# Adding each expert block into the output rows in DRAM, in place of a combination behind the blocks

## The reference, cut to what matters

```
g_sel = argmax(g_logits)                       # 1 of 4 groups
top_p, top_i = top_k(softmax(e_logits), 2)     # 2 of the group's 8 experts
top_w = g_gate * top_p / sum(top_p)
...                                            # assignments sorted by expert, padded to blocks of 128 rows
def expert_rows(xb, e):
    hid = silu(xb @ w_gate[e]) * (xb @ w_up[e])      # 1024 -> 512
    return hid @ w_down[e]                           # 512 -> 1024
y_rows = map(expert_rows, x_rows, block_expert)
y = zeros.at[row_token].add(y_rows * row_weight)     # every token is in two blocks
out = h + y
```

## Time and profile before

| | |
|---|---|
| median of three runs | 1733.02 us |
| profiled execution | 1731.12 us, span 1729.0 us |
| mean granted TensorE clock | 0.962 |
| busy share of the span | PE 93%, DVE 72%, ACT 37%, POOL 21% |
| expert blocks | about 1061 to 1691 us |
| combination (L1622 to L1626) | about 1691 to 1729 us |

### The profile page before, as it was taken

One profiled execution on the slowest core, in us unless ns is written; L12 is line 12 of the kernel. 1 busy time (PEld: TensorE's weight loads), 2 busy tenths in 40 slices (PEclk: granted clock), 3 DMA queues, 4 the chain that ended last, 5 costly groups with the idle time before them and its releaser, 6 DMA issues. The chain is left out here.

```text
span 1729.0 us, 25257 instructions
## 1 busy us (share of the span) xinstructions
PE 1599.6 (93%) x7334; PEld 1254.7 (73%) x7334; DVE 1253.2 (72%) x2272; ACT 640.1 (37%) x1075; POOL 360.5 (21%) x495
## 2 busy tenths in 40 slices
PE   6999999999999999999998854999999999999991
PEld 5778888788888788888887744667766776677660
DVE  6658878768688587787786747767776777677655
ACT  5333232223232322332322412545554555455430
POOL 2221121221221211303221011222122212211210
PEclk9999999999999999999999966999999999999996
DMA  4221221221221211212213533799999999999927
GB/s 149 52 74 44 56 68 44 56 68 33 66 55 56 62 36 51 73 38 68 56 49 122 211 127 103 285 358 353 359 370 353 355 364 359 348 346 349 356 101 297
DMA packets 138508, 292.62 MB, mean 169 GB/s; under 512 B 17920, under 2 KB 68528, under 8 KB 137392
## 3 DMA queue, kind: packets, MB, share of 16 engines
q1 hardware_dynamic: 129056, 274.68, 45.7%
q0 software_dynamic: 9360, 16.80, 2.7%
HBM read 283.42 MB, written 25.30 MB: 179 GB/s over the span
## 5 line engine op out<-in xcount | busy, mean ns | idle before, releaser
L1691 ACT ACTIVATE gu_hi<-w_gu 128x1024 fp32r<-128x1024 f32 x256 | 272.6, 1066 | 311.3 <-PE g_ps L1734 247.4
L1788 DVE TENSOR_TENSOR gu_lo<-w_gu,gu_hi 128x1024 fp32r<-128x1024 f32 x256 | 313.4, 1225 | 90.6 <-ACT gu_hi L1691 67.2
L1027 PE MATMUL proj<-uTh,wl 128*128 128x512 f32 x768 | 309.6, 403 | 6.9 <-issue 6.9
L1029 PE MATMUL proj<-uTh,wh 128*128 128x512 f32 x768 | 301.8, 393 | 0.0
L1028 PE MATMUL proj<-uTl,wh 128*128 128x512 f32 x768 | 301.5, 393 | 0.0
L1752 PE MATMUL y<-w_d,hT 128*128 128x512 f32 x512 | 225.1, 592 | 1.0 <-DVE hT L1814 1.0
L450 POOL TENSOR_TENSOR wl<-raw,wh 128x512 fp32r<-128x512 f32 x96 | 128.7, 1358 | 393.1 <-ACT wh L511 393.1
L1752 PEld LDWEIGHTS y<-w_d,hT 128*128 128x128 f32 x512 | 94.9, 190 | 108.4 <-issue 107.1
L1027 PEld LDWEIGHTS proj<-uTh,wl 128*128 128x128 f32 x768 | 145.8, 190 | 37.3 <-issue 7.5
L1029 PEld LDWEIGHTS proj<-uTh,wh 128*128 128x128 f32 x768 | 145.4, 189 | 31.6
L1028 PEld LDWEIGHTS proj<-uTl,wh 128*128 128x128 f32 x768 | 145.8, 190 | 28.7
(11 more groups left out here) (244 smaller groups left out, 2733.8 us busy)
## 6 DMA issues: line engine op xcount, KB each, us to landing
w_gu<-in_moe_w_gate_dram SPq DMA_DIRECT2D x128, 512.0 KB, 8.8
w_gu<-in_moe_w_up_dram SPq DMA_DIRECT2D x128, 512.0 KB, 9.2
w_d<-in_moe_w_down_dram SPq DMA_DIRECT2D x128, 512.0 KB, 5.6
raw<-in_ssd_w_in_dram SPq DMA_DIRECT2D x96, 256.0 KB, 3.5
E<-acum_dram SPq DMA_DIRECT2D x64, 256.0 KB, 3.6
raw<-in_ssd_w_out_dram SPq DMA_DIRECT2D x32, 256.0 KB, 3.0
w_gu<-y_dram SPq DMA_DIRECT2D x8, 1024.0 KB, 9.8
hacc<-in_x_dram SPq DMA_DIRECT2D x8, 512.0 KB, 7.2
```

What stands on the lines that cost most here:

```text
L1027: nc.tensor.matmul(out, al, bh, start=start, stop=False)
L1029: return nc.tensor.matmul(out, ah, bh, start=False, stop=stop)
L1691: nc.scalar.activation(wh[:, j % RING, :], weights.gate_up(b, j), ACT.Copy).then_inc(w_hi, 1)
L1788: vec.tensor_tensor(wl[:, j % RING, :], weights.gate_up(b, j), wh[:, j % RING, :].bitcast(F32), ALU.subtract).then_inc(w_lo, 1)
```

## The change: rows are fetched, added to and stored back, block by block

- `routing` gets `hacc` and `out`, and SP stores the eight tiles of `hacc` to `out` there, ahead of the eight down-weight loads. `ridx` keeps one index per row, the token; the second value carried through the table is now the row's weight (`wrow`).
- A new `fetch` on GpSimd reads block m's rows of `out` into `yb` by an indirect DMA. Its index operations come right behind the scatter of block m-1; the DMA waits until that scatter has landed, since both blocks may hold the same token.
- `y_out` becomes two additions `yb = y * wrow + yb`, waits for the fetch, and moves in VectorE's program: block m's now stands in the pass of block m+2, behind the low parts of pieces 4 to 7. In the last pair the one of block 30 stands ahead of the last `hT` copy, the one of block 31 at the very end.
- `scatter` writes `yb` to the rows of `out`. The combination is gone; the program ends when the last scatters have landed.

```
 def routing(...):
         def _(sp):
             ...
+            ov = out.rearrange("(i p) d -> p i d", p=P)
+            for i in range(NT):
+                sp.dma_start(ov[:, i, :], hacc[:, i, :]).then_inc(out_stored, 16)
             ...
+            g.memset(yb[:], 0.0).then_inc(const_steps, 1)
-            link(vec.tensor_tensor(wtok[:, 0, :], s8[:, 3, :], s8[:, 10, :], ALU.mult))
-            link(vec.tensor_tensor(wtok[:, 1, :], wtok[:, 0, :], s8[:, 7, :], ALU.mult))
+            link(vec.tensor_tensor(src[:, 0, :, 1], s8[:, 3, :], s8[:, 10, :], ALU.mult))
+            link(vec.tensor_tensor(src[:, 1, :, 1], src[:, 0, :, 1], s8[:, 7, :], ALU.mult))
             for k in range(2):
                 link(vec.tensor_scalar(src[:, k, :, 0], toki[:], -PADROW, None, ALU.add))
-                link(vec.tensor_scalar(src[:, k, :, 1], toki[:], 2.0, k - PADROW, ALU.mult, ALU.add))
...
-            link(vec.tensor_scalar(ridx[:], tab_ps[:], PADROW, None, ALU.add))
+            link(vec.tensor_scalar(ridx[:], tab_ps[:, 0, :], PADROW, None, ALU.add))
+            link(vec.tensor_copy(wrow[:], tab_ps[:, 1, :]))
 def experts(...):
             last = pairs(sp, body, peeled=2)
             load_down(last, 1)
-            for b in range(2):
-                sp.wait_ge(scattered[b], val(last, 0, 8, 16))
-            ...                                  # loads of y_dram, stores of hacc
-            def scatter(p, b):
-                wait(pool, scattered[b], p, 0, 8, 0)
-                g.tensor_copy(stmp[:, b, :], ridx[:, 1, bass.ds(val(p, b, 1, 0), 1)]).then_inc(sidx_done, 1)
+            def fetch(p, b):
+                g.tensor_copy(stmp[:, b, :], ridx[:, bass.ds(val(p, b, 1, 0), 1)]).then_inc(sidx_done, 1)
                 wait(pool, sidx_done, p, b, 3, 1)
-                wait(pool, y_done, p, b, 2, 2)
                 g.tensor_tensor(sidx[:, b, :], stmp[:, b, :], zero[:], ALU.add).then_inc(sidx_done, 1)
                 wait(pool, sidx_done, p, b, 3, 2)
+                if b == 1:
+                    wait(pool, scattered[0], p, 0, 8, 16)
+                else:
+                    wait(pool, scattered[1], p, 0, 8, 0)
                 g.tensor_tensor(held[:, 1, :], zero[:], zero[:], ALU.add).then_inc(sidx_done, 1)
-                g.indirect_dma_start(y_dram, bass.IndirectOffsetOnAxis(sidx[:, b, :].bitcast(U32), 0), yb[:, b, :], None,
-                                     bounds_check=last_row, oob_is_err=False).then_inc(scattered[b], 16)
+                g.indirect_dma_start(yb[:, b, :], None, out, bass.IndirectOffsetOnAxis(sidx[:, b, :].bitcast(U32), 0),
+                                     bounds_check=last_token, oob_is_err=False).then_inc(fetched[b], 16)
+            def scatter(p, b):
+                wait(pool, y_done, p, b, 2, 2)
+                g.tensor_tensor(held[:, 2, :], zero[:], zero[:], ALU.add).then_inc(held_done, 1)
+                g.indirect_dma_start(out, bass.IndirectOffsetOnAxis(sidx[:, b, :].bitcast(U32), 0), yb[:, b, :], None,
+                                     bounds_check=last_token, oob_is_err=False).then_inc(scattered[b], 16)
...
                         scatter(shifted(p, -1), 1)
+                    fetch(p, b)
...
             def y_out(p, b):
-                wait(dve, scattered[b], p, 0, 8, 0)
+                wait(dve, fetched[b], p, 0, 8, 16)
                 for j in range(2):
                     wait(dve, y_mm, p, b, 2, j + 1)
-                    vec.tensor_copy(yb[:, b, j * 512:(j + 1) * 512], y_ps[j][:]).then_inc(y_done, 1)
+                    rows = yb[:, b, j * 512:(j + 1) * 512]
+                    vec.scalar_tensor_tensor(rows, y_ps[j][:], wrow[:, bass.ds(val(p, b, 1, 0), 1)], rows,
+                                             ALU.mult, ALU.add).then_inc(y_done, 1)
             def body(p, last):
                 for b in range(2):
                     for j in range(RING, 8):
                         split(p, b, j)
+                    if p[0] is not None or p[1]:
+                        y_out(shifted(p, -1), b)
...
-                    if b == 1:
+                    if b == 1 and last:
                         y_out(p, 0)
-                    elif p[0] is not None or p[1]:
-                        y_out(shifted(p, -1), 1)
...
-            for i in range(NT):                  # additions into hacc
-                ...
```

More of the change, by code:

```diff
@@ L1224, in _, with routing @@
                 logits(k)
-def routing(nc, lg, ridx, etab, npairs, wtok, weights, xg, zero, ident, b_group, b_expert):
+def routing(nc, hacc, lg, ridx, wrow, etab, npairs, weights, xg, yb, zero, ident, b_group, b_expert, out, out_stored):
     NT = lg.shape[1]
@@ L1485, in _, with experts @@
             dve.wait_ge(tab_mm, 2 * NT)
-            link(vec.tensor_scalar(ridx[:], tab_ps[:], PADROW, None, ALU.add))
-def experts(nc, hacc, ridx, etab, npairs, wtok, weights, xg, zero, ident, u2_dram, y_dram, out):
+            link(vec.tensor_scalar(ridx[:], tab_ps[:, 0, :], PADROW, None, ALU.add))
+            link(vec.tensor_copy(wrow[:], tab_ps[:, 1, :]))
+def experts(nc, T, ridx, wrow, etab, npairs, weights, xg, yb, zero, ident, u2_dram, out, out_stored):
     _, D, FF = weights.src[0].shape
@@ L1497, in experts @@
     KF = FF // P
-    NT = hacc.shape[1]
-    T = NT * P
+    NT = T // P
     RING = 4
@@ L1522, in experts @@
         stmp = sb("stmp", [P, 2, 1], I32)
-        held = sb("held", [P, 2, 1], I32)
+        held = sb("held", [P, 3, 1], I32)
         tp = [psum(f"tp3_{j}", [P, 4, P]) for j in range(2)]
@@ L1528, in experts @@
         y_ps = [psum(f"y3_{j}", [P, 512]) for j in range(2)]
-        y2 = [weights.gu[j // 2][:].rearrange("p a k f -> p (a k f)")[:, (j % 2) * 2 * D:(j % 2 + 1) * 2 * D]
-              .rearrange("p (c d) -> p c d", c=2) for j in range(4)]
         w_hi = sem("w_hi3")
@@ L1538, in experts @@
         sidx_done = sem("sidx_done")
+        held_done = sem("held_done")
         gathered = [sem(f"gathered{b}") for b in range(2)]
+        fetched = [sem(f"fetched{b}") for b in range(2)]
         scattered = [sem(f"scattered{b}") for b in range(2)]
@@ L1549, in experts @@
         y_done = sem("y_done3")
-        y2_loaded = [sem(f"y2_loaded{j}") for j in range(4)]
-        comb = sem("comb")
-        out_stored = sem("out_stored")
         def val(p, b, per, add):
@@ L1630, in _ @@
             g = nc.gpsimd
-            last_token, last_row = pool.to_reg(T - 1), pool.to_reg(2 * T - 1)
+            last_token = pool.to_reg(T - 1)
             def gather(p, b, ahead):
@@ L1638, in gather @@
                 wait(pool, turned, p, b, 2, 2 * (ahead - 1))
-                g.tensor_copy(gtmp[:, par, :], ridx[:, 0, bass.ds(val(p, b, 1, ahead), 1)]).then_inc(gidx_done, 1)
+                g.tensor_copy(gtmp[:, par, :], ridx[:, bass.ds(val(p, b, 1, ahead), 1)]).then_inc(gidx_done, 1)
                 wait(pool, gidx_done, p, b, 3, 3 * ahead + 1)
@@ L1668, in body @@
                         scatter(shifted(p, -1), 1)
+                    fetch(p, b)
             for ahead in range(3):
                 gather(FIRST, 0, ahead)
+            pool.wait_ge(out_stored, 16 * NT)
             last = pairs(pool, body, peeled=2)
@@ L1675, in _ @@
             pool.wait_ge(gathered[0], val(last, 0, 8, 32))
+            for b in range(2):
+                pool.wait_ge(scattered[b], val(last, 0, 8, 16))
         @block.scalar
@@ L1819, in _ @@
             y_out(pairs(dve, body, peeled=2), 1)
-            for i in range(NT):
-                dve.wait_ge(y2_loaded[i % 4], 16 * (i // 4 + 1))
-                for c in range(2):
-                    if c:
-                        dve.wait_ge(comb, 2 * i + 1)
-                    vec.scalar_tensor_tensor(hacc[:, i, :], y2[i % 4][:, c, :], wtok[:, c, i:i + 1], hacc[:, i, :],
-                                             ALU.mult, ALU.add).then_inc(comb, 1)
 def layer(nc, x, norm_mix, norm_ffn, ssd_w_in, ssd_conv_w, ssd_conv_b, ssd_dt_bias, ssd_a_log, ssd_d, ssd_norm,
@@ L1846, in layer @@
         xg = ctx.enter_context(nc.sbuf_tensor("xg", [P, 2, D], F32))
+        yb = ctx.enter_context(nc.sbuf_tensor("yb", [P, 2, D], F32))
+        out_stored = ctx.enter_context(nc.semaphore("out_stored"))
         zero = ctx.enter_context(nc.sbuf_tensor("zero", [P, 1], I32))
         ident = ctx.enter_context(nc.sbuf_tensor("ident2", [P, P], F32))
-        routing(nc, lg, ridx, etab, npairs, wtok, weights, xg, zero, ident, moe_b_group[0], moe_b_expert[0])
-        experts(nc, hacc, ridx, etab, npairs, wtok, weights, xg, zero, ident, u2_dram, y_dram, out[0])
+        routing(nc, hacc, lg, ridx, wrow, etab, npairs, weights, xg, yb, zero, ident, moe_b_group[0], moe_b_expert[0],
+                out[0], out_stored)
+        experts(nc, T, ridx, wrow, etab, npairs, weights, xg, yb, zero, ident, u2_dram, out[0], out_stored)
 _INS = ["x", "norm_mix", "norm_ffn", "ssd_w_in", "ssd_conv_w", "ssd_conv_b", "ssd_dt_bias", "ssd_a_log", "ssd_d",
```

8 lines of the change are left out of this document (3 added, 5 removed).

## The result

| | before | changed |
|---|---|---|
| median | 1732.64 us (20 runs, 1728.51 to 1736.33) | 1739.02 us (20 runs, 19 of them 1731.09 to 1745.94) |
| profiled execution | 1731.12 us, span 1729.0 | 1732.48 us, span 1730.7 |
| mean period of the additions, blocks 1 to 26 | 19.15 us (TensorE's pass) | 20.26 us |
| last `y` product starts | 1683.28 us | 1709.51 us |

The ratio is 1.0032, with a 95% interval of 1.0019 to 1.0044. I had forecast 1702 us, a gain; the time lies outside the range. One run of the changed kernel stands apart, at 5881.53 us: it is left out of the ratio and of the range, and without it the median is 1738.95. The changed kernel's runs also spread more than those of before (15 us against 8, without that one), and its profiled execution is the second shortest of them, 6.5 us under the median.

A forecast was written before the change was run, and what follows sets the result against it. TensorE was taken to bound the blocks, with 38 us of combination behind them. Removing it, with a hidden ring, a new tail and 0.3 less routing, gave span 1698.1 against 1729.0, gain 30.9, median 1702 us; range 1697 to 1728.

The forecast's parts named there:

- The bound: In the blocks: TensorE, busy 198.00 of 198.00 us, sets the 19.15 us pass; behind them 38 us of combination without matmuls.
- the ring: Once per block: additions, scatter, next fetch, next additions; length L 18.32 us, under the 19.15 us pass, so no cost.
- the price of a microsecond (28 us): In the blocks: each microsecond of L over 19.15 costs 28 us, for 28 blocks beside weight loads, less 1.94 once.
- fetch: the same form as the gather, median 6.5: Last transfer of the loop: the fetch lands after 6.5 us, the gathers' median of 4.5 / 6.5 / 7.6.
- the other four terms: Rest of the loop: additions 1.49, to scatter's instruction 1.59, to fetch's `held` 8.19, to fetch's instruction 0.50 us.
- the first rival: Blocks: fetch issued at the pass's start takes 8.1, L 19.9, 20 us lost, time 1722; chance 0.20 for binding in part.
- the 16.6 at which the prediction said that the whole gain goes: Blocks: scatter and fetch landings summing to over 15.5 us cost something; over 16.6 they take the whole gain.
- the slower rival: Blocks: both transfers at slow ends, 10.2 and 7.6, L 21.5, 65 us lost, time 1767; chance 0.12.
- 0.4 to the end: Tail: the span ends 0.4 us after the last scatter lands at 1698.0, so at 1698.4.
- `held` and the additions: In the pass: `held` ahead of the scatter 1.19 us beside low parts; the two additions 1.49 us.
- Routing and the stores: Stage ahead of the blocks: about -0.3 us; the eight `hacc` stores, 10 us, hidden with 11 us to spare.
- VectorE's cover of 1.94 us: In a pass: 1.94 us are left for a late fetch before TensorE stands still.

The follow-up runs named there:

- lengthening the ring: Changed kernel with four more 128x1 POOL operations between the scatter's landing and the fetch; 1767.91 us, ratio 1.0202 to the kernel before.
- other rows: Changed kernel with all its waits, but the fetch reads the same number of rows from `u2_dram`; 1738.58 us, ratio 1.0034 to the kernel before.
- last wait on SyncE: Changed kernel with the waits for the last two scatters on SP instead of POOL, and a 512-byte store behind them; one execution, 1740.04 us.
- gather ahead of the fetch: Changed kernel with POOL's gather of block m+3 moved behind the scatter of m-1, ahead of the fetch of m; 1723.09 us, ratio 0.9941.
- fetch freed: Changed kernel, but the fetch reads `u2_dram` and waits only for its buffer, the scatter of two blocks ago; 1706.92 us, ratio 0.985.
- groups in turn, additions between: Changed kernel with blocks from the four expert groups in turn, fetch waiting for the scatter of m-2 up to block 27; 1707.11 us, ratio 0.9871.
- `hid` and longer: Changed kernel with additions behind product `hid` in the pass of block m+1 and four added POOL operations before the fetch; 1726.75 us, ratio 0.997.
- four groups in turn, with the additions behind `hid`: Changed kernel with additions behind `hid`, last waits on SP, blocks from the groups in turn, looser fetch wait up to block 27; 1705.70 us, ratio 0.9843.

## Why the prediction was wrong, step by step

- **The bound, and the ring.** Right in kind. The pieces, their order and the price of a microsecond (28 us) are as forecast; freeing the fetch and lengthening the ring show it from both sides. By the prediction's own rule the measured period costs 28 x (20.26 - 19.15) - 1.9 = 29.2 us; 27.4 were found.
- **The step that failed: "fetch: the same form as the gather, median 6.5".** It measures 9.1 with its wake, 2.6 more, while the other four terms came out 0.6 shorter together. L is 20.26 and not 18.32. The row was right for the gather of before, which started 14.0 us into TensorE's pass (a median, counted from the first gate matmul). The fetch starts 2.3 us into it. I had given this as the first rival, with 8.1 for the fetch, and set it aside because the gathers land after 6.5 in a full machine. That argument held the form and the load fixed, but not the moment. The two landings sum to about 17.0 (7.98 - 0.09 + 9.13 - 0.05), over the 16.6 at which the prediction said that the whole gain goes. So the mechanism is the first rival's, stronger than it was priced (9.1 and not 8.1). The time fell into the slower rival's class, over 1736, but not by its mechanism: that one wanted both transfers at their slow ends, 10.2 and 7.6, and the scatter stayed at its median while the fetch went beyond 7.6. With a distance to the bound of 0.8 us and landings that differ by more, a chance of 0.32 for all cases of a binding ring was too small.
- **The second step: "0.4 to the end".** The end of before had that, because 38 us of combination lay behind GpSimd's last DMA. The closing DRAIN, 8.0 us now, was in the trace of before (6.4 us from 1692.0) and I did not ask what would stand beside it. Without it the end is right: from the last `y` product to the landing 1722.2 it is 12.7 us, 13.4 were forecast.
- **`held` and the additions.** 1.09 for 1.19, and 1.41 for 1.49: right. That `held` is long beside low parts is shown by its 0.18 once they are not there. The rule of the Trainium skill that I weighed (SBUF — State Buffer, Who interferes with whom) is that a VectorE operation with two SBUF inputs and a GpSimd operation that reads SBUF exclude each other. These two numbers agree with it. What the forecast left out is that the DMA instructions grow too: beside low parts the scatter's takes 1.83 instead of 1.02, a fetch's or a gather's up to 2.1 instead of 1.04. For the scatter nothing of it reaches the landing (7.98 to the wake with 1.83, 8.33 with 1.02). Fetches with the long instruction do land later in the same kernel (medians 10.0 and 8.6 for blocks 2 to 27, of five and eight landings), but most have the short one and are still 2 us over 6.5.
- **Routing and the stores.** The part forecast at -0.3 measured -0.4: from the start of the first copy in it (1023.36 before, 1021.43 now) to the end of the tables (1059.82, 1057.52) it went from 36.46 to 36.09. The stage ahead of it came 1.9 sooner, which no edit explains; that was luck, on the side of the forecast. The eight stores of `hacc` are hidden: the DMA share from 1045 to 1061 is 0.09.
- **VectorE's cover of 1.94 us.** Right: in the turn shown VectorE waits 2.07 for the fetch and TensorE's down product behind it has no gap.

**The moment, from all kernels.** The traces of the experiments show the fetch at different places in TensorE's pass. Only fetches of blocks 2 to 27 with the short instruction (1.04) and a landing in the profile are counted:

| kernel | fetch starts, us into the pass | landing, median us (fetches) |
|---|---|---|
| changed | 2.3 | 8.6 (8) |
| other rows | 2.4 | 8.6 (9) |
| last wait on SyncE | 2.4 | 8.9 (21) |
| gather ahead of the fetch | 2.5 | 8.3 (21) |
| fetch freed | 14.4 | 7.5 (13) |
| groups in turn, additions between | 14.4 | 7.3 (26) |
| `hid` and longer | 15.3 | 7.3 (26) |

So early in the pass a fetch takes 0.8 to 1.6 us longer than late in it, whichever tensor its rows come from, and with the short instruction alone. The gather behind it makes at most 0.3 of this: it follows after 2.1 us in the quick kernels and after 3.3 in the changed one. In the blocks of four groups in turn, with the additions behind `hid`, the fetch starts at 3.1 with no gather in flight and has a median of 8.5, there with the long instruction. A fetch at 2.3 is issued among the weight loads of gate and up, most of which SyncE issues from 1 to 9 us into the pass in the changed kernel; one at 14.4 is not.

**What stays open.** Why this place makes a transfer long. It is not the rate of the DMA engines: in the 7 us behind the fetch's start they move 325 GB/s in the changed kernel and 358 with the groups in turn and the additions between (means of blocks 2 to 27). The weight loads' place in the pass was not moved by itself. Why the gather of before, at 14.0, took 6.5 and not 7.3 is open too; no fetch travelled beside it. Nor is it shown why most runs of the changed kernel are slower than its profiled one. That `held` could go from ahead of the scatter was not tried.

## What to carry to other kernels

When a change chains two transfers through memory once per iteration, sum the whole ring before counting bytes or busy engines, and take each landing from a transfer that starts at the same moment of the iteration; if the slack is smaller than the spread of one landing, forecast that it binds. Then look for a way to open the ring (here, an order in which neighbouring blocks share no rows), which was worth 32 us here; shortening it by a microsecond was worth the same, but left it on the edge. When work behind the last GpSimd DMA goes, look in the trace of before for what its queue does at the end.

## What the runs showed of the hardware that I had not expected

- GpSimd's closing DRAIN grows with the number of indirect DMAs: 8.0 us behind the end of the last DMA instruction, or behind the last wait if that ends later, in all eleven kernels with 97 of them; 5.4 us with 65 (the kernel without fetches, and the one before, where 1692.0 + 6.37 lies 5.4 behind the scatter's instruction). That would be 0.08 us each, an estimate from two counts only.
- An indirect DMA's landing for the same rows and size had medians from 6.5 to 8.9 us in kernels with full weight traffic, mostly by when in TensorE's pass it was issued (8.3 to 8.9 at 2.3 to 2.5 us, 7.3 to 7.5 at 14.4 to 15.3); with the traffic gone it is 3.2 for a scatter and 4.2 for a fetch.
- A longer DMA instruction on GpSimd (1.83 instead of 1.02) did not make the scatter land later (7.98 to the wake, 8.33 with the short one).
